# Differential attention: joining the two exponentials of a head on VectorE before the transpose, with a fourth logits buffer

## What is computed

```python
def block(args):
    ...
    s = jnp.einsum('bqhmd,bkhmd->bhmqk', qi, k).astype(jnp.float32) * scale + bias[None, :, None]
    p = jax.nn.softmax(s, axis=-1)
    w = p[:, :, 0] - lam * p[:, :, 1]
    return jnp.einsum('bhqk,bkhd->bqhd', w.astype(v.dtype), v)
```

## Time and profile before

| | us |
|---|---|
| median of three runs | 1737.75 |
| the three runs | 1735.06, 1737.75, 1738.11 |
| the profiled execution's own time | 1736.73 |
| its span in the trace | 1734.9 |
| TensorE matmul busy in the span | 1584.0 (91%) |
| VectorE / ScalarE / GpSimd busy | 938.1 / 621.0 / 218.0 |

### The profile page before, as it was taken

The page is one execution under the profiler, slowest core; times in us unless marked ns, Lnnn a source line. Parts: engine busy times, 40 slices in busy tenths (PEclk is TensorE's granted clock), DMA queues, the critical chain, the costliest instruction groups (busy, mean ns, idle before and its releaser), DMA issues.

```text
span 1734.9 us, 27116 instructions
## 1 busy us (share of the span) xinstructions
PE 1584.0 (91%) x10485; PEld 1216.5 (70%) x10485; DVE 938.1 (54%) x1543; ACT 621.0 (36%) x961; POOL 218.0 (13%) x241
## 2 busy tenths in 40 slices
PE   9999999777666677899999999999999999999998
PEld 6788985333223323688888888888888888888886
DVE  5675543111101111577786667777777767577767
ACT  5465441100010010433453653334433444553342
POOL 0232110000000000100015231000110114511000
PEclk9999999988889968999999999999999999999999
DMA  9515488999999999965545055533755445065501
GB/s 396 194 69 162 178 329 359 426 426 426 425 426 426 426 426 427 385 244 188 195 162 197 31 200 202 194 119 134 300 188 196 174 166 195 25 230 195 193 37 49
DMA packets 61100, 421.47 MB, mean 243 GB/s; under 512 B 7024, under 2 KB 16080, under 8 KB 17360
## 3 DMA queue, kind: packets, MB, share of 16 engines
q1 hardware_dynamic: 59280, 409.13, 60.0%
q10 hardware_dynamic: 1728, 11.03, 1.7%
HBM read 419.08 MB, written 1.05 MB: 242 GB/s over the span
## 4 chain that ended last, share of the span: by engine, by line
PE 69%; DMA 16%; SPq 6%; DVE 5%; ACT 2%; issue 2%; POOL 1%; DVEq 0%; ACTq 0%
PE bank L1168 17%; PE bank L1211 12%; DMA ring<-in_we 11%; PE bank L1170 9%; PE bank L2208 7%; SPq L2057 6%; PE bank L2137 5%; DMA more<-in_we 3%; PE bank L2372 2%; PE bank L2234 2%; PE bank L1551 2%; PE bank L2353 2%; PE bank L689 2%; DMA ring<-in_wf 2%; PE bank L1198 1%
## 5 line engine op out<-in xcount | busy, mean ns | idle before, releaser
L1168 PE MATMUL bank<-xhl,whu 128*128 128x512 f32 x1280 | 451.8, 396 | 0.0
L1170 PE MATMUL bank<-xhl,wlu 128*128 128x256 f32 x1280 | 357.5, 279 | 0.0
L1168 PEld LDWEIGHTS bank<-xhl,whu 128*128 128x128 f32 x1280 | 240.3, 188 | 57.8
L1170 PEld LDWEIGHTS bank<-xhl,wlu 128*128 128x128 f32 x1280 | 241.1, 188 | 3.3
L985 DVE TENSOR_TENSOR wlu<-ring,whu 128x2048 fp32r<-128x2048 f32 x84 | 192.5, 2292 | 43.8 <-ACT whu L980 43.8
L980 ACT ACTIVATE whu<-ring 128x2048 fp32r (+1 forms) x88 | 167.2, 1902 | 3.5 <-DMA ring<-in_wf 3.5
L985 DVE TENSOR_TENSOR wld<-ring,whd 128x1024 fp32r<-128x1024 f32 x80 | 98.6, 1233 | 113.3 <-ACT whd L980 113.3
L689 PE MATMUL bank<-ring,xg 128*32 128x256 f32 x1424 | 105.4, 436 | 38.1 <-DMA ring<-in_we 38.1
L980 ACT ACTIVATE whd<-ring 128x1024 fp32r (+1 forms) x80 | 84.8, 1060 | 128.5 <-PE bank L1211 128.5
L1278 ACT ACTIVATE sg<-sg 128x256 f32<-128x256 f32 x80 | 33.5, 418 | 265.8 <-DVE sg L1357 265.8
L2208 PE MATMUL bank<-ring_r,xTh 128*128 128x512 f32 x384 | 109.8, 397 | 4.6 <-DVE ring_r L520 2.5
(11 more groups left out here) (370 smaller groups left out, 2761.5 us busy)
## 6 DMA issues: line engine op xcount, KB each, us to landing
ring<-in_we SPq DMA_DIRECT2D x141, 1024.0 KB, 26.8
ring<-in_wf SPq DMA_DIRECT2D x88, 1536.0 KB, 6.5
ring<-in_w SPq DMA_DIRECT2D x52, 1024.0 KB, 5.1
more<-in_we SPq DMA_DIRECT2D x51, 1024.0 KB, 25.8
ring<-in_w SPq DMA_DIRECT2D x32, 256.0 KB, 3.7
ln<-in_ln ACTq DMA_DIRECT2D x6, 1024.0 KB, 6.0
bias<-in_bias ACTq DMA_DIRECT2D x2, 2048.0 KB, 9.4
bias<-in_bias SPq DMA_DIRECT2D x1, 2048.0 KB, 20.4
```

The lines of the kernel that those rows point to most:

```text
L1168: pe.matmul(into[:].rearrange("p (a s) -> p a s", a=2), whu[p][:, cols], xhl[:, :, k], start=(k == 0), stop=False, skip_group_check=True)
L1170: ins = pe.matmul(into[:, 0:S], wlu[p][:, cols], xh[:, k], start=False, stop=(k == KD - 1), skip_group_check=True)
```

## The change

- The two places of a differential head are one value group. VectorE's new `mix(u, w)` waits for both exponentials, makes 1/d0, 1/d1 and c, and adds c E1 to E0 in place, in two instructions of 128x256. One set of transposes, one ScalarE copy and one product follow, and `output` is one L2589-like instruction for every group.
- There are 16 value groups instead of 20. The semaphores of the transposes, copies, products and outputs count groups; `value_of[u]` is the group of a place. A new semaphore `mix_ok` tells TensorE that a joined block is ready.
- The table of logits buffers has a fourth one, `lg_d`, in the columns of `proj2` that held the queries and keys of the differential heads for the first 128 tokens. `lg_free[u]` is the count of transposed groups that place u's buffer waits for.
- ScalarE's `head(1, ...)`, the high part of the second piece of the mixer's output, is moved from `behind(17)` to `behind(18)`.

```diff
         lg2_c = at("lg2_c", xT_at, [P, NT, S + 1])
-        lg_ring = [lg2[:, 0], lg2[:, 1], lg2_c[:]]
+        lg_d = proj2[:, 0, D0:D0 + NT * S].rearrange("p (t s) -> p t s", t=NT)
...
+        rden4 = small[:, 188:196].rearrange("p (b t) -> p b t", b=4)
...
+        values2 = [(n, n + 1) if unit.half == 0 else (n,) for n, unit in enumerate(units2) if unit.half != 1]
+        value_of = {n: v for v, heads in enumerate(values2) for n in heads}
+        PAIRS2 = sum(len(heads) == 2 for heads in values2)
+        VALUES2 = len(values2)
+        lg_buffers = [lg2[:, 0], lg2[:, 1], lg2_c[:], lg_d]
+        lg_at = [0, 1, 2, 0, *((n - 3) % 4 for n in range(4, UNITS2))]
+        lg_last = [max((m for m in range(n) if lg_at[m] == lg_at[n]), default=None) for n in range(UNITS2)]
+        lg_free = [0 if m is None else value_of[m] + 1 for m in lg_last]
...
-                    if u == 17:
+                    if u == 18:
                         head(1, 0)
                         head(1, 1).then_inc(th_ok, 1)
...
-            def values(u):
-                pe.wait_ge(o_ok, n0 + u - 1)
-                pe_values(pe, u, n0 + u, units[u], 0)
-
-            for u in range(len(units)):
-                if u == 0:
-                    pe.wait_ge(ex_ok, n0)
-                    between(0)
-                    scores(AHEAD2[0])
-                pe.wait_ge(pt_ok, n0 + u - 1)
-                pe.wait_ge(ex_ok, n0 + u + 1)
+            def probs_T(v):
+                u = values2[v][0]
+                pe.wait_ge(pt_ok, v0 + v - 1)
+                if units[u].half is None:
+                    pe.wait_ge(ex_ok, n0 + u + 1)
+                else:
+                    pe.wait_ge(mix_ok, l * PAIRS2 + sum(len(heads) == 2 for heads in values2[:v + 1]))
+                lg = lg_buffers[lg_at[u]]
                 for t in range(NT):
                     for i in range(NT):
-                        ins = pe.transpose(bank[2 + u % 2][:, t * S + i * P:t * S + (i + 1) * P],
-                                           lg_ring[u % 3][:, i, t * P:(t + 1) * P], ident[:])
+                        ins = pe.transpose(bank[2 + v % 2][:, t * S + i * P:t * S + (i + 1) * P], lg[:, i, t * P:(t + 1) * P], ident[:])
                 ins.then_inc(pt_ps, 1)
+
+            def values(v):
+                unit = units[values2[v][0]]
+                pe.wait_ge(o_ok, v0 + v - 1)
+                pe.wait_ge(pt_ok, v0 + v + 1)
+                for i in range(NT):
+                    for t in range(NT):
+                        ins = pe.matmul(bank[4 + v % 2][:, i * unit.dv:(i + 1) * unit.dv], pT_at[:, v % 2, t, tok(i)], unit.v[t],
+                                        start=(t == 0), stop=(t == NT - 1))
+                ins.then_inc(pv_ps, 1)
...
+            pe.wait_ge(ex_ok, n0)
+            between(0)
+            scores(AHEAD2[0])
+            for u, unit in enumerate(units):
+                v = value_of[u]
+                if unit.half != 0:
+                    probs_T(v)
+                if unit.half != 1 and v >= 1:
+                    values(v - 1)
...
-                unit, n, lg = units[u], n0 + u, lg_ring[u % 3]
-                act.wait_ge(lg_ok, n + 1)
-                act.wait_ge(o_ok, n - 3)
-                act.wait_ge(pt_ps, n - 2)
+                unit, lg = units[u], lg_buffers[lg_at[u]]
+                act.wait_ge(lg_ok, n0 + u + 1)
+                if u >= 4:
+                    act.wait_ge(o_ok, v0 + value_of[u - 4] + 1)
+                act.wait_ge(pt_ps, v0 + lg_free[u])
                 for i in range(NT):
...
-                act.wait_ge(pt_ps, n + 1)
-                act.wait_ge(pv_ps, n - 1)
-                act.activation(pT_at[:, b].rearrange("p t s -> p (t s)"), bank[2 + b][:], ACT.Copy).then_inc(pt_ok, 1)
+                if unit.half != 0:
+                    act.wait_ge(pt_ps, v0 + v + 1)
+                    act.wait_ge(pv_ps, v0 + v - 1)
+                    act.activation(pT_at[:, v % 2].rearrange("p t s -> p (t s)"), bank[2 + v % 2][:], ACT.Copy).then_inc(pt_ok, 1)
...
-                st.then(dve.reciprocal(rden[:, u % 2], den4[:, u % 4]))
+                st.then(dve.reciprocal(rden4[:, u % 4], den4[:, u % 4]))
...
-                dve.wait_ge(pt_ps, n - 2)
+                dve.wait_ge(pt_ps, v0 + lg_free[u])
...
-            def output(u):
-                unit, n, b = units[u], n0 + u, u % 2
-                if unit.half == 1:
-                    st.sync()
-                    st.then(dve.tensor_scalar(nrd[:, b], rden[:, b], nlam[:, 0:1], None, ALU.mult))
-                dve.wait_ge(pv_ps, n + 1)
+            def mix(u, w):
+                dve.wait_ge(ex_ok, n0 + w + 1)
+                st.then(dve.reciprocal(rden4[:, u % 4], den4[:, u % 4]))
+                st.link(dve.reciprocal(rden4[:, w % 4], den4[:, w % 4]))
+                st.link(dve.scalar_tensor_tensor(nrd[:, 0], rden4[:, w % 4], nlam[:, 0:1], den4[:, u % 4], ALU.mult, ALU.mult))
+                first, second = (lg_buffers[lg_at[n]] for n in (u, w))
+                for i in range(NT):
+                    ins = dve.scalar_tensor_tensor(first[:, i, 0:S], second[:, i, 0:S], nrd[:, 0, i:i + 1], first[:, i, 0:S],
+                                                   ALU.mult, ALU.add)
+                ins.then_inc(mix_ok, 1)
+
+            def output(v):
+                u = values2[v][0]
+                unit = units[u]
+                dve.wait_ge(pv_ps, v0 + v + 1)
                 st.sync()
-                src = bank[4 + b][:, 0:NT * unit.dv].rearrange("p (i d) -> p i d", i=NT)
-                if unit.half == 1:
-                    dve.wait_ge(o_ok, n)
-                    for i in range(NT):
-                        ins = dve.scalar_tensor_tensor(unit.out[:, i], src[:, i], nrd[:, b, i:i + 1], unit.out[:, i],
-                                                       ALU.mult, ALU.add)
-                        if i < NT - 1:
-                            st.then(ins)
-                else:
-                    ins = dve.tensor_tensor(unit.out, src, bc(rden[:, b], unit.dv), ALU.mult)
-                ins.then_inc(o_ok, 1)
+                src = bank[4 + v % 2][:, 0:NT * unit.dv].rearrange("p (i d) -> p i d", i=NT)
+                dve.tensor_tensor(unit.out, src, bc(rden4[:, u % 4], unit.dv), ALU.mult).then_inc(o_ok, 1)
 
             logits(0)
             after_first()
             logits(1)
             between(0)
             logits(2)
-            for u in range(1, len(units)):
-                inverse(u - 1)
+            for u, unit in enumerate(units):
+                if u == 0:
+                    continue
+                v = value_of[u]
+                if unit.half == 1:
+                    mix(u - 1, u)
+                elif len(values2[v - 1]) == 1:
+                    inverse(u - 1)
                 if u + 2 < len(units):
                     logits(u + 2)
-                output(u - 1)
+                if unit.half != 1:
+                    output(v - 1)
                 between(u)
                 behind(u)
             inverse(len(units) - 1)
-            output(len(units) - 1)
+            output(VALUES2 - 1)
 
         def ret_rows(h, blk):
             r = 64 * (h % 2)
```

More of the change, by code:

```diff
@@ L269, in build @@
         ex_ok = sem("ex_ok")
+        mix_ok = sem("mix_ok")
         pt_ps = sem("pt_ps")
@@ L1693, in before_scores @@
                         pe.wait_ge(t_out, tb + QK_READY[u])
-                pe_heads(pe, units2, l * UNITS2 + UNITS1, between, before_scores, lambda: pe_out_first(pe, run2(l, 1), tb))
-                pe_out(pe, run2(l, 1), tb, (l + 1) * UNITS2 + UNITS1)
+                pe_heads(pe, units2, l, between, before_scores, lambda: pe_out_first(pe, run2(l, 1), tb))
+                pe_out(pe, run2(l, 1), tb, (l + 1) * VALUES2 + UNITS1)
                 pe_ffn(pe, l, 1)
@@ L1749, in behind @@
                         head(2, 1).then_inc(th_ok, 1)
-                act_heads(act, units2, l * UNITS2 + UNITS1, between, behind)
+                act_heads(act, units2, l, between, behind)
                 load_ln(act, l * 3 + 1)
@@ L1906, in tail @@
                     ins.then_inc(t_out, 1)
-                dve_heads(dve, st, units2, l * UNITS2 + UNITS1, between, behind, evacs[2])
+                dve_heads(dve, st, units2, l, between, behind, evacs[2])
                 tail(2)
@@ L2482, in dve_units, with pe_heads @@
             dve_output(dve, st, len(units) - 1, n0 + len(units) - 1, units[-1])
-        def pe_heads(pe, units, n0, between, ready, drain):
+        def pe_heads(pe, units, l, between, ready, drain):
+            n0, v0 = l * UNITS2 + UNITS1, l * VALUES2 + UNITS1
             def scores(heads):
@@ L2490, in scores @@
                     after = units[v].after
[L2491 to L2494, removed]
+                    if after is not None:
+                        pe.wait_ge(ex_ok if units[after].bias is None else lg_ok, n0 + after + 1)
                 pe_scores(pe, [units[v] for v in heads])
-            def values(u):
```

(24 more changed lines are left out.)

19 lines of the change are left out of this document (11 added, 8 removed).

## The result

| | before | after |
|---|---|---|
| median of the runs, us | 1737.28 (1735.06 to 1738.11, 4 runs) | 1758.02 (1756.38 to 1761.26, 4 runs) |
| ratio, 95% interval | | 1.0123 [1.0111, 1.0136] |
| the profiled execution: span, us | 1734.9 | 1754.6 |

What follows compares the result with a forecast made beforehand. TensorE's own stream was taken to bound the heads of the two mixers. With the saved work netted into the chain's delay, 1736.73 + 4.0 (chain) + 2.4 (clock) = 1743.1 us, range 1735 to 1750.

Steps and rivals of the forecast that it cites:

- The join, 1.39 us: VectorE joining a pair's two halves before the transposes, built from kindred instructions: 1.39 us, bounds 0.90 and 1.6.
- The chain, waits of 0.5 and some 2.2 us: Product, output, bringing out, join and transposes in series make TensorE wait in the differential heads: 2.0 us later per layer, 4.0 in all.
- my walk: Step-by-step timing of one layer's differential heads, from 962.42 to the scores of places 14 and 15: 985.57 against 983.54.
- Saved work of 10.2 us: TensorE loses one transpose set and one product per pair, 1.28 us; eight pairs make 10.2 us.
- the join hides: Rival: VectorE delivers the joined block before TensorE needs it, so the whole 10.2 us is gain: 1726.5 us, chance 0.12.
- The clock, 2.4 us: TensorE's clock in the differential heads falls to a mean of 0.94: 1.2 us a layer, 2.4 in all, bounds 0 and 11.
- the clock stays down: Rival: TensorE's clock stays low through most of the differential heads, costing 11 us: 1752 us, chance 0.10.
- `head`'s move and the fourth buffer: ScalarE's moved head copy and the extra logits buffer: each taken at 0, the move with 0.7 us gain per layer as far end.
- the four waits: Sign: TensorE waits for VectorE's join at three transposes a layer, some 2 us each, and 0.5 us at the first.
- The distance from the product at 962.47 to the scores of places 14 and 15: Sign: this stretch of a layer's heads, from the old 962.42, should take about 23 us, not 21.
- TensorE's busy time: Sign: TensorE's busy time in the changed profile should fall by some 10 us while the span grows.

## Why the prediction was half right

- **The join, 1.39 us**: measured 1.39, its two links at 0.04 and 0.03 us. The one of heads 6/7 takes 1.58 us (971.00 to 972.58), with L2606 at 0.33 and L2609 at 0.96.
- **The chain, waits of 0.5 and some 2.2 us**: measured 0.43, 2.44, 2.18 and 2.18. Its price was put at 2.0 us a layer and is 2.66, 5.3 in all instead of 4.0, read where the clock stays up (2.75 up to the scores of places 14 and 15, where my walk ended). The gap is in the links, as far as the changed kernel's rows show it: the product is followed by the next piece after 0.95 us where I took 0.84 (962.47 to 963.42), the join of heads 6/7 took 1.58, and TensorE started 0.15 us after the first join's end (965.21 to 965.36) where I took 0.05.
- **Saved work of 10.2 us**: what I called all gain if TensorE stayed the pace is 5.6 us with no join at all. The rival "the join hides" at 1726.5 us was thus out of reach in this order: 6.1 us under 1736.7 is 1730.6. That a removed product had hidden the bringing out of the `between` piece in front of it was in no part of my working.
- **The clock, 2.4 us: the step that failed.** I took the mean clock of the nearest rows, 0.94, over the 20 us of the walk, and 0.72 there as the upper end, 11 us in all. Measured 15.6 us in the medians, and per layer 4.3 and 9.7 us in the changed kernel's profile (46.47 and 51.87 less 42.16), 9.8 and 0 in the one with zeros in the second layer. Two things were wrong in it. The first is how much of the walk is at the lower level. I had 1.2 us a layer for it; up to the scores of places 14 and 15 the changed kernel lost 2.5 and 5.8 us to the clock (27.41 and 30.75 us from the scores of places 6 and 7, against 24.93 with zeros). The 0.94 came from a stretch whose stands are of another kind, 1.4 us each and waits for DMA; that this is why it misled isn't shown. The second is the span: I ended it with the waits, and counted nothing behind them. The lower level goes on there, and the changed kernel lost another 1.8 and 3.9 us. In the first layer of the kernel with zeros in the second, TensorE is busy throughout for some 12 us behind the last wait and at the lower level, and loses 5.6 us: nearly half a microsecond for each.
- The rival "the clock stays down" (1752 us, chance 0.10) was the right mechanism, and priced too low: I gave it 5.6 us a layer, and two layers lost 9.7 and 9.8. With the measured chain and 9.8 us for each layer it is 1736.7 + 5.3 + 19.6 = 1761.6 us, beside a highest run of 1761.26.
- The Trainium skill, page "TensorE: Matmul & The Clock Gate", section "What's actually happening", says that the low level is the default and activity releases it. The traces agree as far as they go: in the changed kernel the lower level came back in stands of 2.2 to 2.4 us or just behind them. What counts as activity they show less simply: from 990 to 1000 us of the kernel with zeros in the second layer TensorE's busy time was 5.00 of 5.00 us twice, at 0.50.
- **`head`'s move and the fourth buffer**, taken at nothing: no gain or loss shows for either. The wait for the exponential went without a gain, as forecast; that a wait of 0.6 us for `tail` would take its place I had not said.
- Of what should have been seen, the four waits were. The distance from the product at 962.47 to the scores of places 14 and 15, forecast at about 23 us, is 23.9 with zeros and 26.4 and 29.7 in the changed kernel's two layers. TensorE's busy time I said would fall by 10 us, and it rose by 10.7. Of that rise 5.1 us lies in the two layers (81.21 us against 76.14 before, from the scores of places 6 and 7 to the projection), where the same matmuls at the lower level last longer. The other half is not the change's doing: TensorE's busy time from 300 to 700 us, in the mixture of experts, is 285.47 us against 280.35. The kernel without the join, with less work and clock 1.00 in the heads, shows 1585.7 us in all, also more than the 1584.0 of before. So more busy time for less work points to the clock only in the stretch that was changed, not in the page's total.

Open: which stand starts a fall, and how long it lasts. The same instructions lost 4.3, 9.7 and 9.8 us (9.7 and 4.2 with `head` moved back), four zeros in a wait were enough to keep the clock up, and one layer with waits under 0.8 us had a fall; what decides between these was not tried.

## What to carry to other kernels

When a change takes work off a full TensorE and puts a wait there, price three things: the removed work (less what it had covered on other engines), the wait, and the clock, whose lower level outlasts the stands and is paid at half speed by the busy work behind them. Look first at where the new instruction sits in its engine's row: one step earlier on VectorE made waits of 2.2 to 2.4 us into 0.6 to 0.8. Where a wait can't be removed, a few matmuls of zeros in it tell how much of the loss is clock, and can be kept.

## What the runs showed of the hardware that was not expected

- Stands of 2.2 us, three in some 20 us, brought the clock from 1.00 to 0.50 for part of the heads; the same waits with 0.9 us of each filled, leaving 1.2 to 1.5 us, kept it at 1.00 in the profiled execution of both layers.
- The same instructions and waits lost 4.3 us to the clock in one layer and 9.7 in the other, within one execution; with `head` moved back it was 9.7 in the first and 4.2 in the second.
- The clock stayed at 0.50 for some 12 us behind the last wait (988.87 to 1000.6) while TensorE was busy throughout.
- A fall of 3.4 us began in a layer whose waits were all under 0.8 us.
